# Three fused blocks on one core: the second pair's front in tiles of its own, weight remainders first in each slot

## Chip, cores and metric

One core of one Trainium2 chip runs the whole program in one launch. The metric is the device time in microseconds (us); lower is better. TensorE (PE) does matrix products, VectorE (DVE) and ScalarE (ACT) work element by element, SyncE (SP) starts transfers. Each engine takes its instructions in the order of the program and waits on counters (semaphores) for the others.

## What is computed

Two residual layers (gated linear attention with a convolutional feed-forward, then attention with the same) and a third block. The change lies in the third block, which runs a 31-tap causal convolution branch and an RWKV-7 branch on the same projection of the normed input, and mixes them:

```
p = h @ w_in                      # 1024 -> c_val, c_gate, c_og, r, k, v, low ranks, r_og, g_conv, g_rwkv
u = c_val * sigmoid(c_gate);  u = silu(layernorm(causal_conv31(u))) * silu(c_og)
decay = exp(-exp(-softplus(-(w0 + tanh(w_low) @ w2)) - 0.5));  a = sigmoid(a0 + a_low @ a2)
kk = normalise(k * k_k, per head of 64);   k = k * (1 + (a - 1) * k_a)
for t: state = state*decay_t - (state @ kk_t) (kk_t*a_t)^T + v_t k_t^T;   o_t = state @ r_t
o = (groupnorm(o) + sum(r*k*r_k) * v) * silu(r_og)
m = sigmoid(g_conv) * (u @ w_conv_out) + sigmoid(g_rwkv) * (o @ w_rwkv_out);  x = x + gate * (m @ w_out)
```

256 tokens, width 1024, 16 heads of 64; the scan is done in chunks of 64 tokens.

## The kernel before

All activations lie channel by partition. Weights come in **blocks** of 1024 x 256 values (1 MB), one transfer each, into a ring of three buffers `RAW`. Each product is made of three passes with 11-bit parts, so a block is split first: ScalarE writes the high part (`split_hi_half`, L306, two halves), VectorE the **remainder** raw minus high (`split_lo_half`, L314, two halves), and only then may TensorE use it (`unit`, eight units of six matmuls each). The first remainder half waits until both high halves are done (`w_hi_ready`). For the blocks of `LO_IN_RAW` the remainder overwrites the raw block, so the buffer is free for the next load only when the product is done.

The third block is written as **steps** s = -3 to 4 of 13 **slots** r. A **duo** is two **pairs** of heads (128 channels each). In step s the engines interleave: the chunk recurrence of duo s (`chain`), the masked scores and the inversion of a triangular matrix for duo s+1 (`middle`), the preparation of keys and decays of duo s+2 (`front`, first pair, then second), the group norm of duo s-1 (`gn`), and the units of the weight blocks that `STEP_BLOCKS` gives to the step, spread evenly over its slots by `put_blocks`. The convolution's taps (L2757, four or five a slot) run on VectorE through steps -2 to 2; the layer norm (`ln`) and the product with `og` follow in step 3, and `conv_y_hi` and `conv_y_lo` split its result for the block `cout0`.

The inversion ties three engines together. In an even slot TensorE sums (`x_part`, L1279 and L1282) and ScalarE copies the sums to memory (L2079). In the odd slot behind it TensorE multiplies (`y_part`, L1268) and VectorE masks the product (L2908, "the y mask"). The next even slot's `x_part` cannot start before that mask is written (`y_ready`). On each engine a slot's work stands in this order, in step 0 for instance: TensorE hops of `chain`, `x_part` or `y_part` with front pieces in between, then the slot's units; ScalarE `chain`, `middle`, high halves and evacuations (`take_block`), then `front` and `gn`; VectorE `chain`, `middle`, `front`, then remainders, evacuated blocks (`use_block`) and taps, then `gn`.

The second pair's front follows the first's in the same tiles (`AA`, `SIG`, `TMP`, both sigmoids) and the same bank: its decay pieces are in slot 6, its rate pieces in slot 8, its sigmoids on ScalarE in the same slots behind them, its key mixing (`keys_mixed`, L2821 to L2825) in slot 8 and its last products (`keys_decayed`) in slot 11. The sums of squares (`kk_sums`, slot 7) and the bonus sums (`rkrk_sums`, slot 9), both L1143, wait for these. From duo 3's bonus sums on, step 1 slot 5 waits for the first group norm's root (L1518).

## Time and profile before

| | |
|---|---|
| time of three runs | 1060.43, 1060.87, 1064.71 us (median 1060.87) |
| profiled execution | 1062.21 us, its span 1060.4 us |
| mean granted TensorE clock | 0.983 of full |
| busy: TensorE, weight loads, VectorE, ScalarE | 95%, 89%, 82%, 57% |
| third block's steps -2 to 3 | from 623.6 to about 984 us |

The span goes from the first to the last instruction; 1.8 us of the execution lie outside it. A busy share says how much an engine ran, not whether anyone waited for it: what the change can move is read from the waits inside the steps.

### The profile page before, as it was taken

Reading aid. Unit: us, or ns where it says so; the run is one execution under the profiler, and the core shown is the slowest. Engines: PE = TensorE matmul, PEld = TensorE weight load, DVE = VectorE, ACT = ScalarE, POOL = GpSimd, SP = SyncE. Lnnn points to the kernel's source line nnn. Section 1 sums busy time; section 2 is a strip of 40 time slices with the busy share of each in tenths; the row PEclk is TensorE's granted clock in tenths of the full one; section 3 lists DMA queues with packets and bytes.
Section 4 is the critical chain, followed back from the end, with each engine's and each line's share of the span. In section 5 each row is a group of like instructions: output and inputs, shape, how many; then the busy total and the mean of one; then the engine's idle time right before and its main releaser. Section 6 shows DMA issues by size and latency. Waiting matters only on the chain.

```text
span 1060.4 us, 24882 instructions
## 1 busy us (share of the span) xinstructions
PE 1009.8 (95%) x10690; PEld 948.2 (89%) x10690; DVE 867.9 (82%) x1424; ACT 602.3 (57%) x815; POOL 18.3 (2%) x38
## 2 busy tenths in 40 slices
PE   7999999999999999999999998899898899998997
PEld 6999999989899889899999997889888799988996
DVE  7956699889988859999988988999887698855664
ACT  7746664444457648444444677454565466585444
POOL 2000000000000000000000000000000000000000
PEclk9999999999999999999999999999999899999999
DMA  9653367677544416676666353222232223353561
GB/s 284 208 191 120 120 226 243 225 239 233 181 159 160 158 41 218 201 255 228 226 217 201 118 159 120 81 82 82 82 121 82 81 82 103 100 159 121 187 210 40
DMA packets 136074, 168.25 MB, mean 159 GB/s; under 512 B 3216, under 2 KB 125328, under 8 KB 135728
## 3 DMA queue, kind: packets, MB, share of 16 engines
q1 hardware_dynamic: 132080, 153.44, 44.6%
q0 software_dynamic: 3904, 13.50, 3.8%
q8 instruction: 70, 1.15, 0.5%
q14 instruction: 20, 0.16, 0.0%
HBM read 164.83 MB, written 2.10 MB: 157 GB/s over the span
## 4 chain that ended last, share of the span: by engine, by line
PE 68%; DVE 17%; ACT 8%; DMA 3%; issue 3%; SPq 0%; DVEq 0%; ACTq 0%
PE banks L363 13%; PE banks L328 8%; PE banks L329 7%; PE banks L330 7%; PE banks L365 6%; DVE w_parts L288 3%; DVE raw_lo L314 2%; DVE hf L2757 2%; ACT w_parts L306 2%; PE banks L677 2%; PE bank L679 2%; PE bank L677 2%; PE bank L681 2%; PE banks L679 2%; PE banks L681 2%
## 5 line engine op out<-in xcount | busy, mean ns | idle before, releaser
L288 DVE TENSOR_TENSOR w_parts<-raw,w_parts 128x2048 fp32r<-128x2048 f32 x93 | 212.5, 2289 | 27.1 <-ACT w_parts L283 26.7
L363 PE MATMUL banks<-x_parts,w_parts 128*128 128x512 f32 x640 | 227.1, 399 | 0.0
L329 PE MATMUL banks<-x_parts,w_parts 128*128 128x256 f32 x768 | 220.0, 286 | 0.0
L328 PE MATMUL banks<-x_parts,w_parts 128*128 128x256 f32 x704 | 211.7, 301 | 4.5 <-DVE raw_lo L314 4.5
L283 ACT ACTIVATE w_parts<-raw 128x2048 fp32r<-128x2048 f32 x95 | 180.9, 1905 | 3.5 <-PE banks L832 2.1
L365 PE MATMUL banks<-x_parts,w_parts 128*128 128x256 f32 x640 | 179.8, 281 | 0.0
L330 PE MATMUL banks<-x_parts,raw_lo 128*128 128x256 f32 x528 | 151.8, 288 | 0.0
L329 PEld LDWEIGHTS banks<-x_parts,w_parts 128*128 128x128 f32 x768 | 150.2, 196 | 0.5 <-issue 0.5
L328 PEld LDWEIGHTS banks<-x_parts,w_parts 128*128 128x128 f32 x704 | 137.6, 195 | 10.5 <-DVE raw_lo L314 5.1
L363 PEld LDWEIGHTS banks<-x_parts,w_parts 128*128 128x128 f32 x640 | 120.3, 188 | 29.0
L365 PEld LDWEIGHTS banks<-x_parts,w_parts 128*128 128x128 f32 x640 | 120.9, 189 | 0.0
L330 PEld LDWEIGHTS banks<-x_parts,raw_lo 128*128 128x128 f32 x528 | 104.0, 197 | 0.0
L306 ACT ACTIVATE w_parts<-raw 128x1024 fp32r<-128x1024 f32 x86 | 89.7, 1053 | 23.4 <-DMA raw<-in_w_rwkv_out 9.6
L314 DVE TENSOR_TENSOR raw_lo<-raw,w_parts 128x1024 fp32r<-128x1024 f32 x72 | 86.1, 1219 | 18.6 <-ACT w_parts L306 18.6
L2757 DVE SCALAR_TENSOR_TENSOR hf<-big,vecs,hf 128x256 f32<-128x256 f32 x240 | 99.7, 481 | 0.0
L1585 ACT ACTIVATE u<-banks 128x512 f32<-128x512 f32 x40 | 23.9, 599 | 81.9 <-PE banks L365 81.9
L2260 DVE SCALAR_TENSOR_TENSOR big<-u,vecs,big 128x256 f32<-128x256 f32 x168 | 70.1, 480 | 0.0
L1573 ACT ACTIVATE big<-big 128x512 f32<-128x512 f32 x20 | 12.6, 632 | 93.8 <-DVE big L2260 93.8
L677 PE MATMUL banks<-g_parts,w_parts 128*128 128x256 f32 x176 | 50.0, 284 | 1.3 <-DVE g_parts L2338 1.1
L677 PE MATMUL bank<-g_parts,w_parts 128*128 128x256 f32 x176 | 49.8, 283 | 0.0
L679 PE MATMUL bank<-g_parts,w_parts 128*128 128x256 f32 x176 | 49.8, 283 | 0.0
L681 PE MATMUL bank<-g_parts,w_parts 128*128 128x256 f32 x176 | 49.8, 283 | 0.0
(431 smaller groups left out, 2480.6 us busy)
## 6 DMA issues: line engine op xcount, KB each, us to landing
raw<-in_ffn_w_up SPq DMA_DIRECT2D x44, 1024.0 KB, 5.1
raw<-in_w_in SPq DMA_DIRECT2D x36, 1024.0 KB, 5.5
raw<-in_ffn_w_down SPq DMA_DIRECT2D x22, 1024.0 KB, 5.5
big<-in_ada_w_t POOLq DMA_DIRECT2D x24, 512.0 KB, 3.9
raw<-in_gla_w_in SPq DMA_DIRECT2D x11, 1024.0 KB, 5.6
raw<-in_attn_w_qkv SPq DMA_DIRECT2D x6, 1024.0 KB, 4.9
raw<-in_gla_w_out SPq DMA_DIRECT2D x4, 1024.0 KB, 5.6
raw<-in_attn_w_out SPq DMA_DIRECT2D x4, 1024.0 KB, 5.0
```

The costliest lines, as they stand in the source:

```text
L283: nc.scalar.activation(WH[:, n % RING, :, :], RAW[:, n % RING, :, :], ACT.Copy)\
L288: eng.tensor_tensor(w_lo(n), RAW[:, n % RING, :, :], WH[:, n % RING, :, :].bitcast(F32), ALU.subtract).then_inc(w_lo_ready, 1)
L306: ins = nc.scalar.activation(WH[:, n % RING, ks, :], RAW[:, n % RING, ks, :], ACT.Copy)
L314: ins = nc.vector.tensor_tensor(w_lo(n)[:, ks, :], RAW[:, n % RING, ks, :], WH[:, n % RING, ks, :].bitcast(F32), ALU.subtract)
L328: nc.tensor.matmul(ps, wh, xh, start=start, stop=False)
L329: nc.tensor.matmul(ps, wh, xl, start=False, stop=False)
L330: return nc.tensor.matmul(ps, wl, xh, start=False, stop=stop)
L363: nc.tensor.matmul(PS[bank + m].rearrange("p (a t) -> p a t", a=2), WH[:, s, k, ms], XP[:, :, k, :], start=k == 0, stop=False, skip_group_ ...
L365: last = nc.tensor.matmul(PS[bank + m][:, 0:T], WL[:, s, k, ms], XH[:, k, :], start=False, stop=k == KT - 1, skip_group_check=True)
L677: nc.tensor.matmul(ps, wh[:, k, ms], GH[:, gk, :], start=start, stop=False, skip_group_check=True)
L679: nc.tensor.matmul(ps, wh[:, k, ms], GL[:, gk, :], start=False, stop=False, skip_group_check=True)
L2757: ins = v.scalar_tensor_tensor(CONV[:, k, :], U31[:, k, j:j + T], vec("conv_k_2", KT * j + k), CONV[:, k, :], ALU.mult, ALU.add)
```

## The change

1. The second pair gets tiles of its own for rate, decay and squares (`AAS`, `SIGS`, `TMPS`, in constants that are no longer used). Both its pre-activations are computed by TensorE between the scores of slot 1, its two sigmoids by ScalarE in slot 1. Its front moves up: `keys_mixed` to slot 7, `cumulated` to 8, `keys_decayed` to 10. `keys_scaled` of both pairs stands in slots 11 and 12 of the step before.
2. ScalarE's slot order becomes `chain`, `middle`, `front`, `gn`, then high halves and evacuations. VectorE's becomes `chain`, `middle`, remainders, `front`, `gn`, then evacuated blocks and taps.
3. The remainder halves are called for one unit earlier (units 1 and 3 of the block before, not 2 and 4).
4. Blocks 3 to 6 of the third block keep their remainders out of `RAW`; some scratch tiles change place for that.
5. Step 3 has eight blocks, not nine; `cout1` moves into step 4, which spreads three blocks over seven slots instead of two over five.

The pieces of the diff stand in this order: lists and tiles, the calls of the remainder halves, TensorE's scores, ScalarE's `front` and its loop over the slots, VectorE's loop.

```diff
-    3: _blocks("rog2 gc3 og0 og1 og2 og3 rog3 cout0 cout1"),
-    4: _blocks("cout2 cout3 rout0 rout1 rout2 rout3 out0 out1 out2 out3"),
+    3: _blocks("rog2 gc3 og0 og1 og2 og3 rog3 cout0"),
+    4: _blocks("cout1 cout2 cout3 rout0 rout1 rout2 rout3 out0 out1 out2 out3"),
-LO_IN_RAW = range(N_L3 + 3, N_ROUT + 1)
+LO_IN_RAW = range(N_L3 + 7, N_ROUT + 1)
+        TMPS = [TMP, C[:, CC["mask_f"][0]:CC["mask_b"][1]]]
+        SIGS, AAS = [SIG, cst("sin")], [AA, cst("cos")]
...
-                    if u in (2, 4) and n > N_L3 + 3:
-                        put_at(s, q, ("lo", n + 1, u // 2 - 1))
+                    if u in (1, 3) and n > N_L3 + 3:
+                        put_at(s, q, ("lo", n + 1, u // 2))
...
-                decay_piece(2 * d, u, 0)
-                rate_piece(2 * d, u, 6, 0)
+                if p % 2 and u == 0:
+                    pe.wait_ge(sem("sigmoids_ready"), 2 * p)
+                decay_piece(p, u, p % 2 * T)
+                rate_piece(p, u, 6, p % 2 * T)
...
-                elif r == 6:
-                    keys_scaled(second)
+                elif r == 1:
                     decay_sigmoid(second, T)
+                    rate_sigmoid(second, 6, T)
                 elif r == 8:
-                    rate_sigmoid(second, 2, T)
                     kk_root(second)
-                elif r == 10:
+                elif r == 9:
                     decay_exps(second)
...
-                    slot(s, r)
                     if s + 2 < DUOS and (s, r) != (-2, 0):
                         front(s + 2, r)
                     if 1 <= s < DUOS:
                         gn(s - 1, s, r)
...
+                    slot(s, r)
...
+                    remainders(s, r)
                     if s + 2 < DUOS and (s, r) != (-2, 3):
                         front(s + 2, r)
-                    slot(s, r)
                     if 1 <= s < DUOS and r == 5:
                         gn(2 * s - 2, GNS[0])
...
+                    slot(s, r)
```

**ScalarE, step 0, slot 4.** The rows run from the copy of the inversion's sums to the end of the slot. L306 is a high half, L1916 (L1914 in the changed kernel) takes the block `val2`, L1997 and L1998 (L1994, L1995) are the first pair's root with its table load. Before:

```order
L2079 ACTIVATE big<-banks 128x1024 [waits x_summed]
L306 ACTIVATE w_parts<-raw 128x1024 [waits block_done,raw_landed2]
L1916 ACTIVATE big<-banks 128x2x256 [waits zeroed,block_done]
L306 ACTIVATE w_parts<-raw 128x1024
L1513 ACT_TABLE_LOAD
L1997 ACTIVATE big<-big 128x256 [waits kk_sums_kept]
L1998 ACTIVATE big<-big,consts 128x256 [waits act_steps]
```

After:

```order
L2077 ACTIVATE big<-banks 128x1024 [waits x_summed]
L1511 ACT_TABLE_LOAD
L1994 ACTIVATE big<-big 128x256 [waits kk_sums_kept]
L1995 ACTIVATE big<-big,consts 128x256 [waits act_steps]
L306 ACTIVATE w_parts<-raw 128x1024 [waits block_done,raw_landed2]
L1914 ACTIVATE big<-banks 128x2x256 [waits zeroed,block_done]
L306 ACTIVATE w_parts<-raw 128x1024
```

The root and its table load have moved from behind both high halves to ahead of them.

**VectorE, step 0, slots 4 and 5.** `big<-big` in the first rows is `cumulated`, L314 the first remainder half of block `k3`, L2757 the taps, L2919 (L2923) the state update, L2908 (L2912) the y mask of slot 5. Before:

```order
L2829 TENSOR_TENSOR big<-big 128x256 [waits dve_steps]
L2830 TENSOR_TENSOR big<-big 128x256 [waits dve_steps]
L314 TENSOR_TENSOR raw_lo<-raw,w_parts 128x1024 [waits w_hi_ready]
L2757 SCALAR_TENSOR_TENSOR hf<-big,vecs,hf 128x256 [waits dve_steps] x5
L2919 SCALAR_TENSOR_TENSOR att<-att,chunk_decay,banks 128x64 [waits update_summed]
L2919 SCALAR_TENSOR_TENSOR att<-att,chunk_decay,banks 128x64
L2908 TENSOR_TENSOR big<-bank,consts 128x512 [waits y_summed]
```

After:

```order
L314 TENSOR_TENSOR raw_lo<-raw,w_parts 128x1024 [waits w_hi_ready]
L2834 TENSOR_TENSOR big<-big 128x256 [waits dve_steps]
L2835 TENSOR_TENSOR big<-big 128x256 [waits dve_steps]
L2757 SCALAR_TENSOR_TENSOR hf<-big,vecs,hf 128x256 [waits dve_steps] x5
L2923 SCALAR_TENSOR_TENSOR att<-att,chunk_decay,banks 128x64 [waits update_summed]
L2923 SCALAR_TENSOR_TENSOR att<-att,chunk_decay,banks 128x64
L2912 TENSOR_TENSOR big<-bank,consts 128x512 [waits y_summed]
```

The remainder, with its wait for both high halves, now stands ahead of the front's two operations. In slots 6 and 8 of the same step the changed kernel also has a remainder half with this wait at the head; the kernel before has none in these two slots.

**ScalarE, step 3, around the layer norm's root.** L1930 (L1928) takes block `gc3`, L1517 and L1518 (L1515, L1516) are the root, L1944 (L1942) is the table load of the eight silus over the convolution. Before:

```order
L306 ACTIVATE w_parts<-raw 128x1024 [waits block_done,raw_landed1]
L1930 ACT_TABLE_LOAD [waits v_turned,bonus_kept]
L1930 ACTIVATE big<-banks 128x512 [waits block_done]
L306 ACTIVATE w_parts<-raw 128x1024
L1513 ACT_TABLE_LOAD
L1517 ACTIVATE ln_rstd_tile<-bank,consts 128x256 [waits ln_sums]
L1518 ACTIVATE ln_rstd_tile<-ln_rstd_tile 128x256 [waits act_steps]
L2090 ACTIVATE att<-banks 128x128 [waits rhs_summed]
L1944 ACT_TABLE_LOAD
L1944 ACTIVATE hf<-hf,vecs 128x256 [waits ln_on_dve]
```

After:

```order
L1933 ACTIVATE big<-hf 128x2048 [waits ln_on_dve]
L1511 ACT_TABLE_LOAD
L1515 ACTIVATE ln_rstd_tile<-bank,consts 128x256 [waits ln_sums]
L1516 ACTIVATE ln_rstd_tile<-ln_rstd_tile 128x256 [waits act_steps]
L2088 ACTIVATE att<-banks 128x128 [waits rhs_summed]
L306 ACTIVATE w_parts<-raw 128x1024 [waits block_done,raw_landed1]
L1928 ACT_TABLE_LOAD [waits v_turned,bonus_kept]
L1928 ACTIVATE big<-banks 128x512 [waits block_done]
L306 ACTIVATE w_parts<-raw 128x1024
L1942 ACT_TABLE_LOAD
L1942 ACTIVATE hf<-hf,vecs 128x256 [waits ln_on_dve]
```

The high halves of `og1` and the taking of `gc3` with its table load came before the root and now stand between the root and the silus.

## Rows read from the trace of the kernel before

**Rows 1.** Stretches (steps -1, 0 and 2, then one short): us, busy, PEclk, DMA.

```profile
656.10:720.70 64.60, 55.72 (x1041) 51.95 (x1040) 60.90 (x124) 35.14 (x53) 0.00 (x0) 0.95 0.28 84
720.70:790.00 69.30, 64.06 (x1317) 61.11 (x1316) 60.27 (x125) 39.82 (x66) 0.00 (x0) 0.95 0.30 93
...
864.30:919.50 55.20, 54.40 (x1171) 51.65 (x1170) 49.20 (x102) 33.54 (x48) 0.00 (x0) 1.00 0.31 98
...
760.00:762.50 2.50, 2.50 (x18) 2.38 (x15) 2.08 (x4) 0.00 (x0) 0.00 (x0) 0.52 0.00 0
```

The busy columns are PE, PEld, DVE, ACT and POOL, each with its number of instructions; behind them stand the granted TensorE clock as a share of full speed, the busy share of the DMA engines and GB/s.

**Rows 2.** Waits of PE, third block: line <- waited for: total us, times, longest.

```profile
PE banks L1143 <- ACT big L1982: 8.7, 4, 3.2
PE banks L328 <- DVE raw_lo L314: 5.3, 4, 2.9
PE banks L1279 <- DVE big L2908: 4.0, 3, 2.6
...
PE banks L328 <- DVE conv_y_parts L2799: 3.6, 1, 3.6
PE banks L1143 <- DVE big L2823: 3.3, 2, 2.0
```

**Rows 3.** Timeline of PE: starts of `x_part`, steps -1, 0 and 2 (start, us).

```profile
708.52 0.27 PE L1282 MATMUL banks<-big 64*64 64x64 f32 x2
...
716.37 0.33 PE L1282 MATMUL banks<-big 64*64 64x64 f32 x4 [0.49 <-DVE big L2908]
...
741.90 0.22 PE L1282 MATMUL banks<-big 64*64 64x64 f32 x2
...
751.13 0.23 PE L1282 MATMUL banks<-big 64*64 64x64 f32 x2
...
764.45 0.23 PE L1282 MATMUL banks<-big 64*64 64x64 f32 x2
...
908.30 0.22 PE L1282 MATMUL banks<-big 64*64 64x64 f32 x2
...
915.12 1.15 PE L1282 MATMUL banks<-big 64*64 64x64 f32 x32
```

**Rows 4.** Timeline of ACT: high halves of steps -1, 0 and 2, a table load.

```profile
677.38 1.07 ACT L306 ACTIVATE w_parts<-raw 128x1024 fp32r<-128x1024 f32 x1
...
712.79 1.08 ACT L306 ACTIVATE w_parts<-raw 128x1024 fp32r<-128x1024 f32 x1
...
745.42 1.05 ACT L306 ACTIVATE w_parts<-raw 128x1024 fp32r<-128x1024 f32 x1
746.49 1.28 ACT L1513 ACT_TABLE_LOAD   x1
...
756.40 1.05 ACT L306 ACTIVATE w_parts<-raw 128x1024 fp32r<-128x1024 f32 x1
...
913.23 1.05 ACT L306 ACTIVATE w_parts<-raw 128x1024 fp32r<-128x1024 f32 x1
```

**Rows 5.** Timeline of DVE: steps -1 and 0, then step 3's layer norm.

```profile
679.92 0.69 DVE L2908 TENSOR_TENSOR big<-bank,consts 128x512 f32<-128x512 f32 x1
...
746.50 1.23 DVE L314 TENSOR_TENSOR raw_lo<-raw,w_parts 128x1024 fp32r<-128x1024 f32 x1 [0.61 <-ACT w_parts L306]
747.65 2.06 DVE L2757 SCALAR_TENSOR_TENSOR hf<-big,vecs,hf 128x256 f32<-128x256 f32 x5
...
750.01 0.68 DVE L2908 TENSOR_TENSOR big<-bank,consts 128x512 f32<-128x512 f32 x1
...
754.57 0.69 DVE L2847 TENSOR_TENSOR big<-big 128x512 f32<-128x512 f32 x1
...
936.68 2.36 DVE L314 TENSOR_TENSOR raw_lo<-raw,w_parts 128x1024 fp32r<-128x1024 f32 x2 [2.44 <-ACT w_parts L306]
```

**Rows 6.** Timeline of ACT, step 3: table load of the root, and silus.

```profile
936.67 1.28 ACT L1513 ACT_TABLE_LOAD   x1
...
942.25 3.31 ACT L1944 ACTIVATE hf<-hf,vecs 128x256 f32<-128x256 f32 x8 [1.90 <-DVE hf L2786]
```

More of the change, by code:

```diff
@@ L1149, in kk_sums @@
                     pe.wait_ge(sem("kk_squares"), p + 1)
-                    pe.wait_ge(sem("sigmoids_ready"), 2 * p + (1 if p % 2 else 2))
-                last = head_sums(TMP, c, 0)
+                    if p % 2:
+                        pe.wait_ge(sem("bonus_kept"), p)
+                    else:
+                        pe.wait_ge(sem("sigmoids_ready"), 2 * p + 4)
+                last = head_sums(TMPS[p % 2], c, 0)
                 if c == NC - 1:
@@ L1213, in scores @@
                     pe.wait_ge(sem("inverse_ready"), d)
-                fronts = e == 0 and d + 1 < DUOS
-                if fronts:
+                fronts = d + 1 < DUOS
+                if fronts and e == 0:
                     pre_act_ready(d + 1)
@@ L1978, in decay_sigmoid @@
                 act.wait_ge(sem("pre_acts"), 2 * p + 1)
-                if p:
-                    act.wait_ge(sem("kr_exps"), p)
+                if p >= 2:
+                    act.wait_ge(sem("kr_exps"), p - p % 2)
                 table("sigmoid")
-                nc.scalar.activation(SIG, PS[2][:, first:first + T], ACT.Sigmoid, bias=vec("rwkv_w0_2", p))\
+                nc.scalar.activation(SIGS[p % 2], PS[2][:, first:first + T], ACT.Sigmoid, bias=vec("rwkv_w0_2", p))\
                     .then_inc(sem("sigmoids_ready"), 1)
@@ L2106, in _ @@
                 for r in range(SLOTS):
-                    if r == 11 and s + 3 < DUOS:
-                        keys_scaled(2 * (s + 3))
-                        nc.scalar.preload_act_table(ACT.Sigmoid)
-                        loaded[0] = "sigmoid"
                     if 0 <= s < DUOS:
@@ L2123, in _ @@
                         gn_last(r)
+                    if s + 3 < DUOS and r >= 11:
+                        keys_scaled(2 * s + r - 5)
+                        if r == 12:
+                            nc.scalar.preload_act_table(ACT.Sigmoid)
+                            loaded[0] = "sigmoid"
+                    slot(s, r)
                     if 2 <= s and r == 0:
@@ L2788, in ln, with remainders @@
                     ins.then_inc(sem("ln_on_dve"), 1)
-            def slot(s, r):
+            def remainders(s, r):
                 for item in between.get((s, r), ()):
@@ L2793, in slot @@
                         split_lo_half(dve, item[1], item[2])
-                    elif item[0] == "use":
+            def slot(s, r):
+                for item in between.get((s, r), ()):
+                    if item[0] == "use":
                         use_block(item[1])
@@ L2840, in keys_normed @@
                 ch.step(v.tensor_tensor(kk, kk, BB, ALU.mult))
[L2841 removed]
+                ch.done(v.scalar_tensor_tensor(BB, kk, -1.0, AAS[p % 2], ALU.mult, ALU.mult))
             def keys_decayed(p):
@@ L2868, in front @@
                     kk_kept(second)
+                    keys_mixed(second)
                 elif r == 8:
-                    keys_mixed(second)
+                    cumulated(second)
                 elif r == 9:
-                    cumulated(second)
                     bonus(second)
+                    keys_normed(second)
                 elif r == 10:
-                    keys_normed(second)
-                elif r == 11:
                     keys_decayed(second)
```

66 lines of the change are left out of this document (30 added, 36 removed).

## The prediction, made blind

> **What bounds the kernel now.** I read the busy shares first: TensorE is busy nearly throughout (the table above), but the share is an average, so I cut the third block into its steps. In steps -1 and 0 TensorE works 55.72 of 64.60 us and 64.06 of 69.30 us, VectorE 60.90 and 60.27 us, at a mean clock of 0.95; in step 2 the clock is 1.00 and VectorE works 49.20 of 55.20 us [rows 1]. So in the steps that the change touches VectorE has four to nine us to spare, in all thirteen slots together, and whatever makes it stand still there is paid.
>
> Next the chain of waits of TensorE [rows 2]. The second pair's front appears twice: its decay sigmoid comes late (8.7 us in four waits) and its key mixing too (3.3 us in two). The y mask costs 4.0 us in three waits, a remainder 5.3 us in four, the convolution's remainders 3.6 us once. Each of the long waits is followed by a stretch at half clock, 0.52 in a stretch after the wait of 3.2 us [rows 1, 2]. The trace has such a stretch after every wait of 1.6 us or more that I looked at; it lasts some 3.4 us, and at half speed that is 1.7 us of work given away.
>
> Last the cycle that paces the slots. From one `x_part` to the next the order is: sums on TensorE, copy on ScalarE, product on TensorE, y mask on VectorE. In step 0 the starts are 741.90, 751.13 and 764.45, so 9.23 and 13.32 us [rows 3]; the second holds a 3.2 us wait for the sigmoid. In step -1 slot 10 to slot 12 takes 7.85 us, in step 2 6.82 us [rows 3].
>
> **The change part by part.**
>
> *Tiles of its own and TensorE's pieces.* The two kinds of pre-activation pieces of the second pair are the same matmuls as before, moved from slots 6 and 8 into slot 1: no work is added. With both sigmoids in slot 1 the sum of squares no longer waits for a sigmoid; 8.7 + 3.3 us of waits go [rows 2]. If nothing else bound, each loop would be as short as TensorE's own work in it. The remainders of blocks 3 to 6 out of `RAW` free a buffer earlier; the transfers there end before their high halves are due, so I put it at nothing (0.8 us if one of them is late). Work done by ScalarE and VectorE does not change except for three table loads fewer.
>
> *The two slot orders.* What counts is when the y mask is written, since the next even slot waits for it. Now it stands behind this list: ScalarE's copy, its front, both high halves with the taking of a block between them; VectorE's remainder (which waits for both halves), front, evacuated block, taps, the mask. Behind the waiting remainder also stands the update of the state, for which the next hop of the chain on TensorE waits; it is needed later than the mask, so it is not priced apart.
>
> Step 0, slot 4 to 6. Both halves end at 745.42 + 1.05 = 746.47, and the root's table load follows at 746.49 with 1.28 us [rows 4]; with the two activations of the root (0.9 us) that is 2.2 us which now stand ahead of them. VectorE had waited 0.61 us for the second half and started the remainder at 746.50; taps from 747.65, the mask at 750.01 for 0.68 us [rows 5], `x_part` at 751.13. Now the remainder starts near 748.7, then `cumulated` follows it (0.8 us, once done ahead) before the taps: the mask is ready at 750.69 + 2.2 + 0.8 = 753.7, and 11.8 us replace 9.23, **+2.6**.
>
> Step 0, slot 6 to 8. The second half ends at 756.40 + 1.05 = 757.45, 6.3 us behind `x_part` [rows 3, 4]. Behind it come in this order a remainder half (1.15), `keys_decayed` (three operations' worth of 0.69 us, 2.0 [rows 5]), a block in use (0.6), four taps (1.6) and the mask (0.68), 12.3 us in all against 13.3: only **-1.0**, where the wait of 3.2 us was to vanish. Slot 8 to 10 comes by the same list to 0.2 us less, the first slots and the last to 0.5 more. New stalls of TensorE over 1.6 us in both loops give two more stretches at half clock than before; I take 0.8 us for each, since part of the slow work falls where TensorE would wait anyway. Step 0: 2.6 - 1.0 - 0.2 + 0.5 + 1.6, about **+3.4**.
>
> Step 1 has the same slots, but its loops before were already 13 to 15 us long through the wait for the group norm's root, which stays. I take **-0.1**.
>
> Step -1. Slot 2: the second half ends at 677.38 + 1.07 = 678.45 [rows 4]. VectorE would start a remainder there (1.15), then the block in use (0.8) and taps (1.6): the mask starts at 682.0 instead of 679.92 [rows 5], +2.1. Pair 1's bonus sums in step -2 come late too (`keys_mixed` stands behind two remainder halves), which I price at 0.9 between nothing and two: **+3.0**. Slot 10: the second half ends 713.87, 5.3 us behind `x_part` [rows 3, 4]; 1.15 + 2.0 + 0.8 + 1.65 + 0.65 behind it make 11.6 us for 7.85, +3.7, and 0.2 over the other slots: **+3.9**.
>
> Step 2. Slot 10: the second half ends at 914.28, 6.0 us behind `x_part` at 908.30 [rows 3, 4]; a remainder half, four taps and the mask make 9.4 us for 6.82, +2.6. Slot 2, alike but with an earlier second half, is estimated at two thirds of it, +1.7, the rest at -0.2: **+4.1**.
>
> Step 3. The root with its table load (2.2 us) is now ahead of both high halves. VectorE's two remainder halves, which stood at 936.68 for 2.36 us and had waited 2.44 us for those [rows 5], stay ahead of the normalisation, so it begins 2.2 us later, and the silus, which at 942.25 already wait 1.90 us for it [rows 6], do too. With the gate product behind them I take **+3.2** for the start of `cout0` (between +2.2 and +4). It takes the place of the 3.6 us wait for the convolution's remainders rather than adding a second one; the stretch at half clock behind that wait is then shared by other work (**-0.9**), and `cout1` in step 4 gives the first block of `rout` a cover of 8 more units (**-0.8**).
>
> *The remainders one unit earlier.* This would hide the 5.3 us of waits for `raw_lo` [rows 2] if VectorE were free to do them; it isn't, and the call now falls in the slot in which ScalarE writes the second half. It costs what stands above, nothing of its own.
>
> **The sum**: 3.0 + 3.9 + 3.4 - 0.1 + 4.1 + 3.2 - 0.9 - 0.8 = +15.8 us. The profiled execution was 1062.21 us, which gives 1078.0; it lay 1.34 above the median, so the forecast for a median is **1077 us**.
>
> **A rule weighed.** The table load of the root takes 1.28 us, and an activation starts 1.3 us behind its start, at once [rows 4]. The Trainium skill (ScalarE: Activation LUTs, What ACT_TABLE_LOAD costs) gives 1283 ns for the load and some 1380 ns on top for draining the pipe, 2.66 us a switch. The first number agrees; for the second this trace shows no room. If it held, each root that now stands ahead of the halves would delay VectorE by 1.4 us more, with three such places 4 us in all and 1081 us.
>
> **Rivals.**
>
> *Nothing takes the place of the waits.* The other side: 8.7 + 3.3 us [rows 2] and four stretches at half clock (1.7 each) go, 18.8 us, for 1042 us (1032 to 1050). For it: each wait is a full stop of TensorE, and its own work from slot 6 to 8 is 8.4 us. Against: VectorE's list above. It decides if the second high half of slots 4, 6 and 8 is written early enough that mask follows mask within 9.2 us, which means within 3.2 us of `x_part`, where the rows have 4.6 to 6.3.
>
> *Half of each.* The loops lengthen, but the cover is greater than I count: TensorE's units of a slot run under VectorE's wait, and the taps behind the mask drift out. Then gains of 12 and losses of 12 meet, 1062 us (1056 to 1067). For it: in step -1 most slots have no wait of TensorE today. Against: each slot is one closed cycle, and an instruction queue has no way to drift past its mask.
>
> *The change doesn't do what it says*: the second pair's sums still wait because `keys_mixed` (slot 7) sits behind a remainder half. It would take back 3.3 of the gain in the first rival, 1045 to 1047 us, inside the range.
>
> **How the numbers follow.** The loops bind, with the sum above: 0.60, and by itself 1068 (half of it) to 1088 (loops some 2 us longer each in step 0 and 1 too). Half of each: 0.16. Nothing takes their place, in full or with late mixing: 0.24. The range of 8 in 10 has to reach from the first rival to the forecast's upper end: 1041 to 1087. A measurement of this kernel tells about 0.5% (5.3 us) from no change. Faster: 0.24 and a few hundredths of the middle case, 0.27; within: 0.12; slower: 0.61.
>
> **What the profile of the changed kernel would show.** Right: no waits on the decay sigmoid; instead waits of L1279 or L1282 on the y mask of 2 to 3 us in slots 6, 8 and 12 of steps -1, 0 and 2; waits of VectorE's remainder on ScalarE's high half far above the present ones; steps -1, 0 and 2 at 71, 73 and 59 us; a clock of 0.95 or less in step 2 too; silus 2 to 3 us later in their step. Wrong: `x_part` to `x_part` near 9 us in slots 4 to 10 of step 0, or a remainder that starts without a wait at the head of an even slot. The steps by themselves tell which term failed: step 0 prices the root, step -1 slot 10 `keys_decayed`, step 3 the layer norm.

## Result: 38 us slower, beyond the forecast's range

The changed kernel takes 1099.24 us (median of 4 runs, 1097.36 to 1100.52) against 1061.15 us in the same session. The ratio is 1.0354, 95% interval [1.0335, 1.0373]. The forecast was 1077 us with a range of 1041 to 1087: the sign was right, the size less than half. The profiled execution has a span of 1098.7 us for 1060.4.

### The profile after

The page's first lines for the changed kernel: span, and busy time by engine.

```profile
span 1098.7 us, 24884 instructions
PE 1019.5 (93%) x10690; PEld 958.6 (87%) x10690; DVE 866.9 (79%) x1424; ACT 599.0 (55%) x812; POOL 18.3 (2%) x38
```

The work is the same. TensorE is busy for 9.7 us more than the 1009.8 us of before, since more of its matmuls ran at half clock (mean granted clock 0.966 for 0.983). The other 28.6 us of the longer span are time in which TensorE stands. The views by stretch show steps -1 to 2 of the changed kernel; the columns are those of [rows 1].

```profile
659.40:735.10 75.70, 58.64 (x1043) 55.49 (x1041) 61.39 (x127) 37.01 (x56) 0.00 (x0) 0.86 0.19 57
735.10:809.20 74.10, 64.92 (x1313) 61.72 (x1312) 58.88 (x122) 38.91 (x66) 0.00 (x0) 0.93 0.28 87
809.20:886.50 77.30, 67.04 (x1346) 63.64 (x1344) 60.97 (x126) 41.15 (x65) 0.00 (x0) 0.91 0.27 84
886.50:948.00 61.50, 56.06 (x1170) 53.11 (x1168) 46.67 (x94) 31.77 (x46) 0.00 (x0) 0.97 0.27 88
```

Step -1 went from 64.6 to 75.7 us at a clock of 0.86, step 0 from 69.3 to 74.1, step 2 from 55.2 to 61.5 [rows 1]. VectorE, which idled 3.7 us of step -1 and 9.0 of step 0 before, now idles 14 and 15, with nearly the same work: it waits. The waits of TensorE, third block, in the changed kernel:

```profile
PE banks L1276 <- DVE big L2912: 20.4, 9, 3.9
PE banks L1279 <- DVE big L2912: 7.7, 2, 4.7
PE banks L1313 <- DVE att L2923: 6.8, 3, 3.4
PE banks L1218 <- DVE pair_tiles L2906: 5.5, 1, 5.5
PE banks L1147 <- DVE consts L2828: 5.4, 1, 5.4
PE banks L328 <- DVE raw_lo L314: 5.2, 2, 4.1
PE banks L1366 <- ACT big L2092: 4.7, 1, 4.7
PE bank L1355 <- ACT big L2092: 2.8, 1, 2.8
```

The waits for the second pair's sigmoid are gone, as the change says (8.7 us in [rows 2]). The two for its key mixing in steps 0 and 1 (3.3 us) are gone too, but the mixing (L2828) is late once in step -2, and that one wait takes 5.4 us, more than both before. Besides, there stand 28.1 us for the y mask (4.5 before), 6.8 us for the state's update, 5.5 for the score masks, and 7.5 us for ScalarE's copies in the recurrence behind step 2. And behind most of them stands one wait of VectorE:

```profile
DVE raw_lo L314 <- ACT w_parts L306: 81.5, 24, 6.4
```

The same row of the kernel before reads as follows:

```profile
DVE raw_lo L314 <- ACT w_parts L306: 18.6, 14, 3.6
```

The remainders wait 63 us longer for ScalarE's high halves. How one of these waits reaches TensorE is seen in step -1, slots 10 and 11. VectorE and then ScalarE of the changed kernel (start, duration):

```profile
721.94 1.23 DVE L314 TENSOR_TENSOR raw_lo<-raw,w_parts 128x1024 fp32r<-128x1024 f32 x1 [2.49 <-ACT w_parts L306]
723.09 0.69 DVE L2852 TENSOR_TENSOR duo_tiles<-duo_tiles,big 128x512 f32<-128x512 f32 x1
...
725.09 0.87 DVE L2717 SCALAR_TENSOR_TENSOR big<-u,vecs,big 128x256 f32<-128x256 f32 x2
725.88 1.67 DVE L2757 SCALAR_TENSOR_TENSOR hf<-big,vecs,hf 128x256 f32<-128x256 f32 x4
727.47 0.68 DVE L2912 TENSOR_TENSOR big<-bank,consts 128x512 f32<-128x512 f32 x1
```

```profile
717.78 1.02 ACT L2077 ACTIVATE big<-banks 128x1024 f32<-128x1024 f32 x1 [2.18 <-PE banks L1279]
718.70 1.05 ACT L306 ACTIVATE w_parts<-raw 128x1024 fp32r<-128x1024 f32 x1
...
720.84 1.07 ACT L306 ACTIVATE w_parts<-raw 128x1024 fp32r<-128x1024 f32 x1
```

ScalarE's copy depends on TensorE's sums, its second half ends at 721.9, the remainder begins there, and `keys_decayed`, the block's use, the taps and the mask follow in a line. TensorE waits 4.72 us:

```profile
728.20 1.97 PE L1279 MATMUL banks<-big 64*64 64x64 f32 x32 [4.72 <-DVE big L2912]
```

and for the next stretch it runs at half clock (0.50):

```profile
730.00:732.50 2.50, 2.50 (x39) 2.38 (x36) 0.86 (x3) 1.17 (x3) 0.00 (x0) 0.50 0.00 0
```

The loop from 716.55 to 728.20 takes 11.65 us; forecast were 11.6 for 7.85.

### The profile page after: what moved, and what is told of

Same layout as the page of the kernel before. It is cut to its first block, busy times and chain, and to the rows that moved or that the text cites. A ratio compares the mean times of both kernels' runs of the same rounds, so it can differ in the third digit from the quotient of the medians.

```text
span 1098.7 us, 24884 instructions
## 1 busy us (share of the span) xinstructions
PE 1019.5 (93%) x10690; PEld 958.6 (87%) x10690; DVE 866.9 (79%) x1424; ACT 599.0 (55%) x812; POOL 18.3 (2%) x38
## 4 chain that ended last, share of the span: by engine, by line
PE 64%; DVE 19%; ACT 12%; issue 3%; DMA 2%; SPq 0%; DVEq 0%; ACTq 0%
PE banks L363 12%; PE banks L328 7%; PE banks L329 6%; PE banks L330 6%; PE banks L365 6%; ACT w_parts L306 3%; DVE raw_lo L314 3%; DVE hf L2757 3%; DVE w_parts L288 3%; PE banks L679 2%; PE bank L681 2%; PE bank L679 2%; PE bank L683 2%; PE banks L681 2%; PE banks L683 2%
## 5 line engine op out<-in xcount | busy, mean ns | idle before, releaser
L288 DVE TENSOR_TENSOR w_parts<-raw,w_parts 128x2048 fp32r<-128x2048 f32 x95 | 217.0, 2288 | 27.3 <-ACT w_parts L283 26.8
L329 PE MATMUL banks<-x_parts,w_parts 128*128 128x256 f32 x768 | 222.4, 290 | 0.0
L328 PE MATMUL banks<-x_parts,w_parts 128*128 128x256 f32 x704 | 214.5, 305 | 1.1 <-DVE raw_lo L314 1.1
L365 PE MATMUL banks<-x_parts,w_parts 128*128 128x256 f32 x640 | 179.8, 281 | 0.0
L329 PEld LDWEIGHTS banks<-x_parts,w_parts 128*128 128x128 f32 x768 | 153.0, 199 | 0.5 <-issue 0.5
L328 PEld LDWEIGHTS banks<-x_parts,w_parts 128*128 128x128 f32 x704 | 140.5, 200 | 6.9 <-DVE raw_lo L314 1.2
L314 DVE TENSOR_TENSOR raw_lo<-raw,w_parts 128x1024 fp32r<-128x1024 f32 x68 | 81.5, 1220 | 81.6 <-ACT w_parts L306 81.5
L363 PEld LDWEIGHTS banks<-x_parts,w_parts 128*128 128x128 f32 x640 | 120.3, 188 | 29.0
L330 PE MATMUL banks<-x_parts,raw_lo 128*128 128x256 f32 x464 | 135.0, 291 | 0.0
L365 PEld LDWEIGHTS banks<-x_parts,w_parts 128*128 128x128 f32 x640 | 121.0, 189 | 0.0
L306 ACT ACTIVATE w_parts<-raw 128x1024 fp32r<-128x1024 f32 x86 | 89.7, 1051 | 24.8 <-DMA raw<-in_w_rwkv_out 18.1
L2757 DVE SCALAR_TENSOR_TENSOR hf<-big,vecs,hf 128x256 f32<-128x256 f32 x240 | 99.3, 477 | 0.0
L330 PEld LDWEIGHTS banks<-x_parts,raw_lo 128*128 128x128 f32 x464 | 93.2, 201 | 0.0
L330 PE MATMUL banks<-x_parts,w_parts 128*128 128x256 f32 x240 | 68.8, 287 | 0.0
L679 PE MATMUL bank<-g_parts,w_parts 128*128 128x256 f32 x176 | 49.8, 283 | 0.0
L681 PE MATMUL bank<-g_parts,w_parts 128*128 128x256 f32 x176 | 49.8, 283 | 0.0
```

What stands on the lines that cost most here:

```text
L288: eng.tensor_tensor(w_lo(n), RAW[:, n % RING, :, :], WH[:, n % RING, :, :].bitcast(F32), ALU.subtract).then_inc(w_lo_ready, 1)
L306: ins = nc.scalar.activation(WH[:, n % RING, ks, :], RAW[:, n % RING, ks, :], ACT.Copy)
L314: ins = nc.vector.tensor_tensor(w_lo(n)[:, ks, :], RAW[:, n % RING, ks, :], WH[:, n % RING, ks, :].bitcast(F32), ALU.subtract)
L328: nc.tensor.matmul(ps, wh, xh, start=start, stop=False)
L329: nc.tensor.matmul(ps, wh, xl, start=False, stop=False)
L330: return nc.tensor.matmul(ps, wl, xh, start=False, stop=stop)
```

## Experiments

Each kernel takes parts of the change away, or adds parts to the kernel before. Ratios are to the kernel before, run beside them; in us they are taken of 1061.

| kernel | ratio, 95% interval | us |
|---|---|---|
| the change | 1.0354 [1.0335, 1.0373] | +37.6 |
| VectorE's order back | 1.0061 [1.0043, 1.0078] | +6.5 |
| ScalarE's order back | 1.0282 [1.0264, 1.0301] | +29.9 |
| both orders back | 1.0036 [1.0015, 1.0056] | +3.8 |
| calls of the remainders back | 1.0032 [1.0019, 1.0046] | +3.4 |
| cout1 back in step 3 | 1.0361 [1.0339, 1.0383] | +38.3 |
| roots behind the high halves | 1.0339 [1.0317, 1.0361] | +36.0 |
| remainder at the head only if its half is of an earlier slot | 1.0055 [1.0034, 1.0076] | +5.8 |
| tiles, and cout1 in step 4 | 0.9915 [0.9899, 0.9931] | -9.0 |
| tiles only | 0.9885 [0.9867, 0.9904] | -12.2 |
| tiles, VectorE's order | 0.9938 [0.9915, 0.9961] | -6.6 |
| tiles, remainder at the head if ready | 0.9907 [0.9893, 0.9922] | -9.9 |
| tiles, calls at units 3 and 5 | 0.9926 [0.9905, 0.9947] | -7.9 |
| before, early calls | 1.0148 [1.0119, 1.0178] | +15.7 |
| before, VectorE's order | 1.0094 [1.0075, 1.0113] | +10.0 |
| before, VectorE's order and early calls | 1.0261 [1.0243, 1.0280] | +27.7 |

The second table is worked out from the timelines of TensorE, of one profiled execution of each kernel: the start of `x_part` in slot 4 of step -1; the times from `x_part` to `x_part` in step 0, slots 4 to 12 (four loops); the last loop of step 2; the last `x_part` of step 2; and what lies between it and the end of the span.

```
                             first   step 0 loops           s.2 last  last x  behind
before                       680.7    9.1 13.3 13.0  8.3      6.8     915.1   145.3
the change                   688.9   12.3 13.2 14.1  8.4      9.9     942.2   156.5
VectorE's order back         681.5   11.1  9.9 11.5  8.4      9.9     919.1   151.5
ScalarE's order back         685.0    9.7 12.1 12.9  8.4      9.9     934.0   158.3
both orders back             680.7    9.1  9.7 10.6  8.4      9.9     912.1   152.8
calls back                   679.0   11.9  9.3 10.4  9.4      6.8     911.8   152.5
tiles, and cout1 in step 4   678.7    9.2  8.4 11.0  9.1      6.8     904.7   146.4
tiles only                   678.5    9.2  8.4 11.0  9.1      6.8     901.9   144.2
head if ready                683.5   11.1 10.1 11.5  8.4      9.9     919.8   147.3
roots behind                 689.4    9.7 12.2 12.7  8.4      9.9     939.2   158.0
before, early calls          681.5    9.1 13.3 13.1  8.3      9.9     924.1   150.7
before, order and calls      687.1    9.7 14.7 14.3  8.3      9.9     937.2   151.2
```

### The two orders and the calls

VectorE's order back (`-` and `+` against the changed kernel; `slot` also takes the remainders again, in the order of their calls):

```diff
...
-                    remainders(s, r)
                     if s + 2 < DUOS and (s, r) != (-2, 3):
                         front(s + 2, r)
+                    slot(s, r)
                     if 1 <= s < DUOS and r == 5:
                         gn(2 * s - 2, GNS[0])
...
-                    slot(s, r)
```

> The changed kernel with VectorE's slot order put back (front, then remainders, evacuated blocks and taps in the order of their calls, then the group norm); ScalarE's order, the early calls, the tiles and the blocks stay changed. Theory 1 (the loss is the y mask standing behind a remainder that itself waits for the second high half, with front and use of a block behind that): front and group norm run again under the wait for the high half. From slot 6 to 8 of step 0 the loop loses keys_decayed (2.0 us) from behind the half, like slot 10 to 12 of step -1; cumulated (0.8) leaves slot 4. Some 7 to 8 such loops in steps -1 to 2 give 1.5 to 2.5 us each, so about 16 us less than the changed kernel's 1099: 1083 (1076 to 1090). The state update's waits (6.8 us in the changed kernel) go under 3. Rival (ScalarE's order alone is the cause, since the half is late whatever stands around the remainder): 1095 or more, waits of x_part on the mask stay over 20 us.

Measured +6.5 us: the order is worth 31 us of the 38, twice what the theory gave it. Slot 4 of step -1 starts 7.4 us earlier, and the waits of the remainders are half of what they were (43.3 us for 81.5).

ScalarE's order back:

```diff
+                    slot(s, r)
                     if s + 2 < DUOS and (s, r) != (-2, 0):
                         front(s + 2, r)
...
-                    slot(s, r)
```

> The changed kernel with ScalarE's slot order put back (high halves and evacuations ahead of front, group norm and keys_scaled); VectorE's order stays changed. Theory 1: both orders share the loss; the root with its table load (2.2 us) leaves the loops of slot 4 and 8 in steps -1, 0, 1 and the group norm's root those of steps 1 and 2, some 6 loops by 2 us: 1087 (1080 to 1093). Rival (ScalarE's order alone is the cause): 1065 or below, and VectorE's waits for L306 back from 81 to under 25 us. Rival (VectorE's order alone): 1095 or more.

+29.9 us: ScalarE's order is worth 8 us here, and 3 us once VectorE's is back (+6.5 against +3.8, intervals that overlap). Neither rival holds; the sizes lie on the side of VectorE's. Half of the 8 us, 3.9, lies ahead of slot 4 of step -1.

> Both slot orders put back; tiles of its own, early calls of the remainders and the block moved to step 4 stay. Theory 1 (the two orders are the cause of the slot loops, the early calls cost nothing by themselves): the loops return to TensorE's own length, 1099 - 16 - 12 - what both share, about 1058 (1050 to 1066). Rival (the early calls make the remainder meet the second half in its own slot): still 1070 or more. Rival (the layout, the pieces of both pairs in slot 1 or the moved block cost): 1075 or more, with the waits in slots 0 to 2 of steps -2 and -1 (5.5 and 5.4 us) and in step 3 kept.

+3.8 us (1065), above the forecast 1058 but inside its range, and below both rivals. Steps -1 to 2 are now 3 us shorter than before (912.1 for 915.1), but the last loop of step 2 is still 9.9 us for 6.8, and 7.5 us are lost behind it. So something beside the orders costs.

The calls of the remainder halves back:

```diff
-                    if u in (1, 3) and n > N_L3 + 3:
-                        put_at(s, q, ("lo", n + 1, u // 2))
+                    if u in (2, 4) and n > N_L3 + 3:
+                        put_at(s, q, ("lo", n + 1, u // 2 - 1))
```

> The changed kernel with the remainder halves called at units 2 and 4 of the block before instead of 1 and 3; both new slot orders stay. The first halves then fall mostly in the slot behind the one in which ScalarE writes the second high half, behind its y mask. Theory 1 with the early calls as a needed part: VectorE's waits for L306 fall from 81 to about 35 us, x_part's waits for the mask from 28 to about 14: 1076 (1068 to 1084). Rival (the orders alone do it, calls a unit earlier or later change little): 1092 or more.

+3.4 us: moving the calls back by one unit, with both new orders kept, has 34 of the 38 us back, more than the 23 that the theory gave it. Either the order or the calls undone gives nearly the whole; they are not two costs that add up.

### What is left when all of them are back

These three keep the second pair's tiles, its earlier front and the layout (these were not taken apart); the calls and ScalarE's order are put back as above, VectorE's order in the first two, and in all but the first `cout1` goes back:

```diff
-    3: _blocks("rog2 gc3 og0 og1 og2 og3 rog3 cout0"),
+    3: _blocks("rog2 gc3 og0 og1 og2 og3 rog3 cout0 cout1"),
...
-        put_blocks(4, STEP_BLOCKS[4][:3], 14)
+        put_blocks(4, STEP_BLOCKS[4][:2], 10)
```

> Both slot orders and the calls of the remainder halves put back; of the change there stay the second pair's tiles with its earlier front, the layout, and cout1 in step 4. Theory 1 (tiles gain, orders with early calls lose): the loops of steps -1 to 2 are as with both orders back or shorter, the last x_part of step 2 by 905 us (915 in the kernel before, 912 with both orders back). Theory 2 (moving cout1 makes step 3 denser around the layer norm and costs 7 us behind step 2): the rest takes 152 us as in the four runs so far, 1057 us in all. Rival to theory 2 (the 7 us come from the early calls too): the rest takes 145 to 147 us, 1051.

> As the one above, and cout1 back in step 3: only the second pair's tiles and its earlier front, with the layout. Theory 1 and 2: the last x_part of step 2 by 905 us, and 145 us behind it: 1050 us, 12 us faster than the kernel before. Rival (the front in slot 1 costs as much as it saves, since the waits for the sigmoid only covered other waits): 1058 to 1064.

> Tiles and earlier front with VectorE's new order, and all else back (ScalarE's order, calls at units 2 and 4, cout1 in step 3). Theory 1: a remainder at the head of a slot costs only where its second high half is written in the same slot; with the old calls that is slots 2 and 4 of the steps, 2 to 5 us in all over tiles only: 1054 (1050 to 1058). Rival (VectorE's order costs by itself, whenever a remainder waits): 1065 or more. Rival (it gains, since remainders come earlier and L328's waits vanish): below tiles only by 2 or more.

Tiles only: 12.2 us faster than the kernel before, the fastest of all that ran (1048.54 us, median of 6, 1047.11 to 1050.63). The loop from slot 6 to 8 of step 0 takes 8.4 us for 13.3: the wait for the sigmoid was no cover for another. Its waits of TensorE, the first rows:

```profile
PE banks L328 <- DVE raw_lo L314: 6.1, 6, 2.0
PE banks L1276 <- DVE big L2909: 5.7, 4, 2.6
PE banks L328 <- DVE conv_y_parts L2799: 3.7, 1, 3.7
PE banks L1147 <- ACT w_r L1516: 3.2, 1, 3.2
PE banks L1279 <- DVE big L2909: 2.6, 2, 1.8
```

The 12.0 us for sigmoid and mixing are gone, and half as much came in their place: the mask costs 8.3 us (4.5 before), remainders 7.3 (5.3), the score masks 2.4 (0.9), and all waits in the third block sum to 27.6 us for 33.5. The rest of the gain is the clock: TensorE is busy 1000.4 us for 1009.8, with the same matmuls. With `cout1` in step 4 it is 3.2 us slower, though the two intervals overlap at their edges; behind step 2 it is 2.2 us longer, so theory 2 (7 us for the move) falls and its rival stands. Both orders put back and the calls still early was +3.8: the early calls alone cost 12.8 us. VectorE's order on the tiles, with the old calls, costs 5.6 us, as forecast (1054).

> The changed kernel with cout1 back in step 3 (nine blocks) and two blocks in step 4; all else changed. Theory 2 (the move costs 7 of the 38 us behind step 2): 1092 (1089 to 1095), behind the last x_part of step 2 149 us instead of 156.5. Rival (the 11 us behind step 2 come from the orders: the layer norm's root waits at ScalarE's head for its sums, 2.57 us, and the high halves behind it are late): 1097 or more.

+38.3 us, the same as the change (1.0361 and 1.0354). In the changed kernel `cout1`'s place makes no difference; theory 2 is wrong here too. The 11 us behind step 2 belong to orders and calls. The rival names the right parts but the wrong path: with `cout1` back the root comes behind both high halves, as in the kernel before, and waits for nothing, while 155.5 us still lie behind step 2.

### Which remainders do it

A remainder goes to the head of the slot only if its second high half is written in an earlier slot:

```diff
             def remainders(s, r):
                 for item in between.get((s, r), ()):
-                    if item[0] == "lo":
+                    if item[0] == "lo" and ("hi", item[1], 1) not in between[s, r]:
                         split_lo_half(dve, item[1], item[2])
```

and the others are taken in `slot`, behind front and group norm.

> The changed kernel, but a remainder half goes to the head of VectorE's slot only if its second high half is written in an earlier slot; one whose second high half falls in the same slot stays behind front and group norm, in the place of its call. Theory (the 28 to 30 us of VectorE's order come from exactly those remainders that wait at the head for a half of the same slot): all of them are had back, 1070 (1066 to 1074), as with VectorE's old order. Rival (every remainder at the head delays the mask, ready or not): 1080 or more.

+5.8 us: all 31 us of VectorE's order are had back, with the early calls and the rest of that order in place. The cause of the order's cost is thereby narrowed to the remainders that meet a high half of their own slot. Its waits of VectorE, the first rows:

```profile
DVE raw_lo L314 <- ACT w_parts L306: 42.6, 17, 6.1
DVE big L2717 <- ACT big L1909: 16.7, 7, 4.9
```

Half of the waiting for high halves remains, but it lies behind the front and no longer ahead of it.

The roots alone behind the high halves, on the changed kernel:

```diff
                     if s + 2 < DUOS and (s, r) != (-2, 0):
-                        front(s + 2, r)
-                    if 1 <= s < DUOS:
+                        if r not in (4, 8):
+                            front(s + 2, r)
+                    if 1 <= s < DUOS and r not in (4, gn_second(s)):
                         gn(s - 1, s, r)
...
                     slot(s, r)
+                    if s + 2 < DUOS and r in (4, 8):
+                        front(s + 2, r)
+                    if 1 <= s < DUOS and r in (4, gn_second(s)):
+                        gn(s - 1, s, r)
```

> The changed kernel with only the roots (keys in slots 4 and 8, group norm in slot 4 and its second slot) put back behind the high halves on ScalarE; all else of its order stays changed. Theory (the roots with their table loads, 2.2 us each, are what ScalarE's order costs): as with ScalarE's whole order back, 1093 (1090 to 1096). Rival (the sigmoids of slots 0 and 1 and the exponentials, which stand ahead too, are the cost): 1097 or more.

+36.0 us, 1.6 us less than the change: the theory fell. The loop from slot 4 to 6 of step 0 does go from 12.3 to 9.7 us, as the forecast's arithmetic had it, but the two loops behind it gain only 1.0 and 1.4 us, and before slot 4 of step -1 and behind step 2 there is a small loss (0.5 and 1.5). What else of ScalarE's order costs its 8 us was not tried. The timeline of ScalarE in the changed kernel offers one place, in step -1 ahead of slot 0: `keys_scaled` now stands ahead of a high half and waits there itself, 5.03 us for VectorE's `keys_decayed`.

```profile
662.72 0.51 ACT L1970 ACTIVATE big<-big,vecs 128x256 f32<-128x256 f32 x1 [5.03 <-DVE big L2858]
663.14 0.49 ACT L1971 ACTIVATE consts<-big,vecs 128x256 f32<-128x256 f32 x1
663.65 1.28 ACT L2121 ACT_TABLE_LOAD   x1
664.94 1.06 ACT L306 ACTIVATE w_parts<-raw 128x1024 fp32r<-128x1024 f32 x1
```

The high half and the taking of the block behind it reach VectorE late, and TensorE then waits 5.5 us for the score masks; with ScalarE's whole order back that wait is 2.9 us. So either engine waits at the head of its slot for the other.

### The same parts on the kernel before

The early calls alone, by the edit of the change:

```diff
-                    if u in (2, 4) and n > N_L3 + 3:
-                        put_at(s, q, ("lo", n + 1, u // 2 - 1))
+                    if u in (1, 3) and n > N_L3 + 3:
+                        put_at(s, q, ("lo", n + 1, u // 2))
```

> The kernel before with the remainder halves called at units 1 and 3; nothing else. Theory (an early call puts the remainder, with its wait, in the slot of its second high half and ahead of that slot's taps and the next mask, whatever the tiles are): as between the runs with both orders back and with the calls back as well, 13 us: 1074 (1069 to 1078). Rival (the cost was made by the shorter loops of the tiles and hides under the sigmoid's waits here): 1063 to 1066.

+15.7 us, as forecast (1074): the early calls cost as much without the tiles. The other way round, a unit later, on tiles only (`+` against units 1 and 3):

```diff
+                    if u in (3, 5) and n > N_L3 + 3:
+                        put_at(s, q, ("lo", n + 1, u // 2 - 1))
```

> Tiles only (1048.5), with the remainder halves called a unit later, at units 3 and 5. Theory (a remainder that no longer meets its high half in its slot frees VectorE): the remaining waits for L306 fall, x_part's waits for the mask too, 2 to 4 us less: 1045. Rival (the blocks' first matmul then waits for the remainder, 5.3 us of that kind stood in the kernel before): 1052 or more.

4.3 us slower than tiles only (-7.9): the waits for remainders ahead of a block's first matmul rose from 6.1 to 14.7 us, while those for the mask fell from 8.3 to 4.1, as the theory had it. Units 2 and 4 are the best of the three.

VectorE's new order on the kernel before, by the edit of the change in its loop over the slots, first without and then with the early calls:

> The kernel before with VectorE's new slot order alone. Theory (the order costs where a remainder meets the second high half of its own slot; with the old calls these are few): 6 us as with the tiles, 1067 (1064 to 1071). Rival (the order is harmless without the early calls, the 6 us belonged to the tiles' shorter loops): 1060 to 1063.

+10.0 us: the order costs by itself, more than forecast.

> The kernel before with VectorE's new slot order and the early calls, nothing else. Theory (order and calls together are the loss, whatever the tiles and ScalarE's order are): calls 15 and the order on top of them 24 to 30: 1103 (1098 to 1107). Rival (the sigmoid's waits of the kernel before cover part of the late masks): 1085 to 1092. Rival (it needs ScalarE's order): 1080 or less.

+27.7 us, where the two alone give 15.7 + 10.0 = 25.7. On the kernel before the two costs just add; on top of the tiles they make 38.9 us (ScalarE's order back, against tiles and `cout1`) for 12.8 and 5.6. The first rival's time came out; that the sigmoid's waits are the cover is argued from where they lie: they are still there, and in the same loops.

```profile
PE banks L1143 <- ACT big L1982: 10.6, 4, 3.3
PE banks L1279 <- DVE big L2911: 6.6, 4, 2.7
PE banks L1282 <- DVE big L2911: 6.5, 2, 3.5
```

The mask costs 13.1 us in waits here against the change's 28.1, and its loops in slots 6 to 10 of step 0 (14.7 and 14.3 us) are at least as long as the change's (13.2 and 14.1), though they began at 13.3 and 13.0 where tiles only has 8.4 and 11.0.

Last, tiles only with the condition on the high half shown above:

> Tiles only, and a remainder half goes to the head of VectorE's slot if its second high half was written in an earlier slot, else it stays in its place. Theory (only the waiting ones cost, 6 us in the run with the whole order): at most 1 us from tiles only, 1048.5 (1046 to 1050), below it if L328's six waits (6.1 us) shrink. Rival (a remainder at the head delays front or chain whether it waits or not): 1052 or more.

-9.9 us, 2.3 us above tiles only, with intervals that overlap; the time (1051) lies between the theory's range and the rival. Ready remainders at the head cost little, but they gain nothing.

## Why the prediction was wrong

In steps -1 to 2 the mechanism is the one forecast: the y mask stands behind a remainder that waits for its high half. The steps that failed are the price of nothing for the early calls (12.8 us were measured), and two terms of the sum, what lies behind step 2 (+3.2 - 0.9 - 0.8 = +1.5, measured +11.3) and the start (+3.0, measured +8.2); the loops of steps 0 and 1 were put too low by 7 us. Shifts of the changed kernel against before, from the second table and the loops:

| part | forecast | measured |
|---|---|---|
| up to slot 4 of step -1 | +3.0 | +8.2 |
| rest of step -1, to slot 12 | +3.9 | +3.6 |
| to slot 12 of step 0 | +3.4 | +7.5 |
| to slot 12 of step 1 | -0.1 | +3.0 |
| to slot 12 of step 2 | +4.1 | +4.8 |
| behind it | +1.5 | +11.3 |

**Right.** The list of what stands ahead of the mask, and its lengths: slot 10 of step -1 11.65 us (11.6), slot 4 of step 0 12.3 (11.8), slot 10 of step 2 9.9 (9.4). The waits for the second pair's sigmoid disappear, and the mask takes their place. The cycle of [rows 3] is what binds. A half clock follows most long waits, but not each: of TensorE's 16 waits of 1.6 us or more in the third block of the changed kernel, 13 are followed by one, and those of 2.57 us (ahead of 796.5), 1.72 and 1.65 are not. The stretch behind the first of these (busy TensorE, granted clock, DMA):

```profile
796.50:800.00 3.50, 3.49 (x84) 1.00 0.02 5
```

Of the signs, the waits of the remainders and the mask came as said, but some of them reach 3.9 and 4.7 us, not 2 to 3, and the clock of step 2 is 0.97, not 0.95 or less.

**The loops between were put too low.** Slots 6 to 8 and 8 to 10 of step 0 were forecast at 12.3 and 12.8 and came at 13.2 and 14.1. In the first VectorE's remainder started at 776.29, 7.1 us behind `x_part` and not 6.3, since ScalarE's copy before it began later too: that `x_part` runs at half clock, behind a wait of 2.7 us for the state's update; in step 1 two loops are 12.5 and 12.3 for 10.9 and 9.4, where the forecast had called the step even. It took step 1 as covered by the group norm's root, which covers only one loop of it (15.2 before, 14.5 after).

**"It is needed later than the mask, so it is not priced apart"**: the update of the state. Three hops of the chain waited 6.8 us for it. It stands on VectorE behind the same remainder.

**The start** (+3.0 for +8.2). Step -2 and slot 0 of step -1 were priced by one wait of 0.9 us. They hold two waits of TensorE of 5.4 and 5.5 us, for the key mixing and the score masks; the second comes by the chain above, from `keys_scaled` over the high half and the block's taking to VectorE. In the kernel before, the longest wait of this stretch was 2.9 us.

**"It takes the place of the 3.6 us wait"** (step 3, +1.5 for +11.3) is the largest. The silus were forecast 2.3 us late in their step and came 4.8 late, and the recurrence was not looked at. In the changed kernel the root of the layer norm waits for its sums on TensorE, the high halves behind it are late, VectorE's two remainders wait 6.13 us for them, and ScalarE's silus 4.30 us for VectorE, with the recurrence's copy behind the silus:

```profile
963.64 0.47 ACT L1515 ACTIVATE ln_rstd_tile<-bank,consts 128x256 f32<-128x256 f32 x1 [2.57 <-PE bank L1100]
...
967.47 1.05 ACT L306 ACTIVATE w_parts<-raw 128x1024 fp32r<-128x1024 f32 x1
...
974.11 3.30 ACT L1942 ACTIVATE hf<-hf,vecs 128x256 f32<-128x256 f32 x8 [4.30 <-DVE hf L2786]
977.32 0.25 ACT L2092 ACTIVATE big<-banks 128x128 f32<-128x128 f32 x1
```

```profile
968.55 2.36 DVE L314 TENSOR_TENSOR raw_lo<-raw,w_parts 128x1024 fp32r<-128x1024 f32 x2 [6.13 <-ACT w_parts L306]
```

In the kernel before the root met sums that were there and the silus waited 1.90 us [rows 6]. TensorE waits 4.74 us for the copy at 977.32, and once more for this copy, 2.79 us, later.

The runs show that this chain is not the whole of it, and that its head is not made by the slot orders. The root stands ahead of these high halves in every run with `cout1` in step 4, with ScalarE's old order too (it waits 2.27 us there, and 158.3 us lie behind step 2); with `cout1` back in step 3 it stands behind them, the waits for the copy are gone, and VectorE's remainders wait 9.56 us elsewhere: 155.5 us. And the wait of 4.74 us is also in the run with a remainder at the head only if its half is ready, where only 147.3 us lie behind step 2:

```profile
955.20 0.69 PE L1366 MATMUL banks<-duo_tiles 64*64 64x64 f32 x8 [4.74 <-ACT big L2092]
```

What that run saves against the change is the second wait for the copy (2.8 us), 3.5 us of waits for remainders and 3.3 us of TensorE's busy time. So most of the loss behind step 2, 9.2 of 11.3 us, goes with the remainders that wait at the head, on more than one path. Why VectorE's old order has only 5.0 of it back stays open. The forecast's -0.8 for `cout1` did not come: its move costs 3.2 us on the tiles, and nothing in the changed kernel.

**"It costs what stands above, nothing of its own"**: the early calls. They cost 12.8 us even with both orders back, and 15.7 us on the kernel before: the remainder's wait then stands ahead of its slot's taps and so ahead of the next mask, whatever stands behind it. The last loop of step 2 shows it cleanly: 9.9 us in all nine kernels with the early calls, 6.8 in all eight without, whatever the orders are. The forecast had put this loop down to the orders. That the calls put the remainder into its high half's slot was in the forecast's text; that this alone has a price was not.

**ScalarE's root** was the first term of the forecast, 2.2 us in slot 4. The loop confirms it (12.3 to 9.7 us with the root behind), the total does not (1.6 us). ScalarE's whole order is worth 3 to 8 us; the rest of the loss comes from VectorE's order and the calls together.

**The rivals.** "Nothing takes the place of the waits" gave 18.8 us for the tiles, 12.0 of waits and 6.8 for the clock; alone they give 12.2. That this equals the 12.0 is chance: in the profiled execution, 14.3 us shorter, TensorE stands 4.9 us less and is busy 9.4 us less. As a forecast of the change it was wrong: it needed the second high half within 3.2 us of `x_part`; in slot 6 of step 0 it ends 7.1 us behind. "Half of each" rested on cover under TensorE's units; there was none. Late mixing occurred once, in step -2, for 5.4 us. By the Trainium skill (ScalarE: Activation LUTs, What ACT_TABLE_LOAD costs) each root would take 1.4 us more than the 1.3 us that rows show. The change has the same 1.28 us and an activation right behind (663.65, then 664.94), so the missing 22 us are not there.

The range ended at 1087 because loops were allowed 2 us more only in steps 0 and 1. The parts that had been put at nothing or at one wait (the start, step 1, all behind step 2) hold 18 of the 22 us that were missed; the rest is in step 0, with the update's waits.

## What to carry to other kernels

An instruction that waits for another engine may be moved ahead in an in-order queue only if that engine has done its part in an earlier slot; here one condition in the planner had 31 us of the loss back. Moving the ready ones ahead gained nothing either (-9.9 us for -12.2 without). A bundle of edits should be taken apart before it is judged: one part of this one, the second pair's tiles with its earlier front and layout, is 12 us faster alone, and is lost in a bundle that is 38 us slower. When a wait is placed at the head of a slot, price every dependent behind it (update, masks, copies of the other chain), also in the slots that had slack before: the parts put at nothing or at one wait missed 18 us, nearly half of the loss.

## What was not expected of the hardware

Nothing new of the chip itself. The half clock weighed more than forecast: the change's step -1 has a mean granted clock of 0.86, and the 9.7 us that TensorE is busy longer with the same matmuls are a quarter of the whole loss. The stretches at half clock also get longer: behind the wait of 4.72 us one reaches from 727.2 to 734.0.
